# Output-projection weight sums: added in SBUF by accumulating DMAs, in place of DRAM

## The chip, the cores and the metric

One core of one Trainium2 chip. The metric is the device time of one launch in microseconds; the kernel before was run three times. All times in the trace are counted from the first instruction of one profiled execution.

## What is computed

A trunk of two layers on a residual stream h of 512 tokens by 2048 channels, all in float32:

```python
u = rms_norm(h, g_norm)
proj = u @ w_in                      # 2048 x 4096
...
y = jnp.concatenate([y_main, y_mem], axis=-1)     # 512 x 2048
h = h + y @ w_out                    # 2048 x 2048, in both layers
```

Layer A's main branch is a gated linear recurrence, layer B's is stick-breaking attention; both have a memory branch of four heads. Between them keys and values are projected from h. The change is in `y @ w_out` alone, with `w_out_a` in layer one (s = 0 in the code) and `w_out_b` in layer two (s = 1).

## The kernel before

Every float32 matmul is made of three passes over float32r operands: each operand is split in a high part (a rounding copy) and a low part (the rest), and TensorE adds high x high, high x low and low x high in PSUM (`three_passes`, L2126 to L2128).

The output projection uses products of sums instead of eight plain quadrant products. `w_out` is cut in two column pairs (n = 0, 1); each pair is a 2048 x 1024 matrix of quadrants b11, b12, b21, b22, each 1024 x 512. Beside the quadrants it needs four sums: t1 = b11 + b12, t2 = t1 + b22, t3 = b12 + b22, t4 = t2 + b21. Seven products per pair, each over two **slabs** of 512 x 512 weights (1 MB), make N_PROJ = 28 slabs per layer, 14 per pair, numbered u. The sums over the y tiles are made by VectorE in SBUF (`y_sum`, L1388).

Weight sums: in the GpSimd program, before its other work and again behind the V stores, `move` (L618) issues DRAM-to-DRAM DMAs, four of 512 KB for each 2 MB matrix, some plain and some accumulating, into `weight_sums`. For one pair they come in a fixed order: t1 and t3 get copies of b11 and b12, then b12 and b22 are added; t2 is copied from t1 and gets b22; t4 is copied from t2 and gets b21. GpSimd waits for `sums_made` between dependent steps. Two pairs, n = 0 and 1, are made in the first layer's time, n = 2 and 3 in the second's.

Slab loads: `load_proj` (L519) on SyncE's queue (SP) loads slab u, already a quadrant or a finished sum, in 2 KB rows (L533) to one of five raw slots of SBUF, by

```python
RAW = [(0, 1, 0, 1, 3, 4)[u] if u < 6 else (2, 3, 0, 1)[(u - 6) % 4] for u in range(N_PROJ)]
proj_raw = [w_raw[:, 0], w_raw[:, 1], four(5), four(6), four(1)]
```

Slots 0 and 1 are `w_raw`, the others parts of `work`. From slab 7 on a load waits until VectorE has finished (`lo_ready`) slab u - 4 (u - 3 for slab 7), the one that held its slot. `load_out` (L539) writes out the order of SP's queue: y tiles (`load_quad`, L537) stand between the slabs, slab 2 waits for the pair's sums, slab 14 for those of the second pair.

For each slab ScalarE (ACT) copies raw to `w_hi` in two halves (`proj_split`, L751; L755), once TensorE is done with slab u - 2, whose `w_hi` and `w_lo` it overwrites; VectorE (DVE) subtracts to `w_lo` (L1367, L1372); TensorE (PE) runs 24 matmuls. Both queues have other work between slabs, in a fixed order: splits of y tiles (L761, L1379), the residual's loads (issued by ACT, L1007 from in_x in layer one, L1246 from h_scratch in layer two), and the additions that drain PSUM. The h^T and V stores of the following stage are also on GpSimd's queue (`store_ht`, L625).

Of the kernel before, what the change touches and what calls it, by code (L numbers as in the profile page):

```python
# [51 lines left out]
RAW = [(0, 1, 0, 1, 3, 4)[u] if u < 6 else (2, 3, 0, 1)[(u - 6) % 4] for u in range(N_PROJ)]  # L52
# [25 lines left out]
def raw_loads(s, u):  # L78

    return s * RAW.count(RAW[u]) + RAW[:u + 1].count(RAW[u])  # L80

# [28 lines left out]
def trunk(nc, x, x_t, mem, mem_t, gain_cols, chan_cols, w_mem_kv, w_in_a, w_rec_gate, w_in_gate,  # L110
# [5 lines left out]
    wa, woa, wb, wob = w_in_a[0], w_out_a[0], w_in_b[0], w_out_b[0]  # L116
# [5 lines left out]
    sums_dram = nc.dram_tensor("weight_sums", [4, 4, KQ * P, C], F32, kind="Internal").ap()  # L122

    def weights(s, n):

        w = (woa, wob)[s]
        b11, b12, b21, b22 = (w[KQ * P * r:KQ * P * (r + 1), C * (2 * n + c):C * (2 * n + c + 1)]
                              for r in range(2) for c in range(2))
        return (b11, b12, b21, b22, *(sums_dram[2 * s + n, m] for m in range(4)))
# [15 lines left out]
    with ExitStack() as ctx:  # L145
# [3 lines left out]
        def sem(name):  # L149
            return ctx.enter_context(nc.semaphore(name))  # L150
# [37 lines left out]
        def four(n):  # L188
            return block(n).rearrange("p (b t) -> p b t", b=4)
# [37 lines left out]
        proj_raw = [w_raw[:, 0], w_raw[:, 1], four(5), four(6), four(1)]  # L227
# [199 lines left out]
        proj_loaded = [sem(f"proj_loaded{n}") for n in range(5)]  # L427
# [3 lines left out]
        sums_made = [sem(f"sums_made{n}") for n in range(4)]  # L431
# [16 lines left out]
        def _(sp):  # L448
# [70 lines left out]
            def load_proj(s, u):  # L519
                b11, _, b21, b22, t1, t2, t3, t4 = weights(s, u // 14)  # L520
                if u < 14:
                    w, c = ((b11, 0), (b11, 1), (t3, 0), (t3, 1), (b21, 0), (t4, 0), (b21, 1), (t4, 1),
                            (t1, 0), (t1, 1), (t2, 0), (t2, 1), (b22, 0), (b22, 1))[u]
                else:
                    order = ((t1, t3, b11, t2, b22, b21, t4), (t1, t2, b22, b11, b21, t3, t4))[s]
                    w, c = order[(u - 14) // 2], u % 2
# [6 lines left out]
                sp.dma_start(proj_raw[RAW[u]], w[C * c:C * (c + 1), :].rearrange("(k p) n -> p k n", p=P)  # L533
                             ).then_inc(proj_loaded[RAW[u]], 16)

# [3 lines left out]
            def load_out(s, y):  # L539
# [11 lines left out]
                sp.wait_ge(sums_made[2 * s], 16 * 32)  # L551
# [5 lines left out]
                load_proj(s, 5)  # L557
# [5 lines left out]
                sp.wait_ge(sums_made[2 * s + 1], 16 * 32)  # L563
# [39 lines left out]
        def _(pool):  # L603
# [48 lines left out]
            for n in range(4):  # L652
                b11, b12, b21, b22, t1, t2, t3, t4 = weights(n // 2, n % 2)
                if n == 2:
                    for c in range(2):
                        store_ht(c)
                    store_ht(3)
                    store_ht(2)
                    pool.wait_ge(h_squares, 12)
                    pool.wait_ge(h_stored, 48)  # L660
                    load_sums(0)
                    load_sums(1)
                    for step in range(KQ):
                        store_sums(step)
                    for m in range(4):
                        store_value(m)
                move(n, t1, b11, ALU.bypass)
                move(n, t3, b12, ALU.bypass)
                pool.wait_ge(sums_made[n], 16 * 8)
                move(n, t1, b12, ALU.add)  # L670
                move(n, t3, b22, ALU.add)
                pool.wait_ge(sums_made[n], 16 * 16)
                move(n, t2, t1, ALU.bypass)
                pool.wait_ge(sums_made[n], 16 * 20)
                move(n, t2, b22, ALU.add)
                pool.wait_ge(sums_made[n], 16 * 24)
                move(n, t4, t2, ALU.bypass)
                pool.wait_ge(sums_made[n], 16 * 28)
                move(n, t4, b21, ALU.add)
# [3 lines left out]
        def _(act):  # L683
# [67 lines left out]
            def proj_split(s, u):  # L751
                act.wait_ge(slab_done, U_PROJ[s] + u - 1)
                act.wait_ge(proj_loaded[RAW[u]], 16 * raw_loads(s, u))
                for k in (0, 2):
                    nc.scalar.activation(w_hi[:, u % 2, k:k + 2, :], proj_raw[RAW[u]][:, k:k + 2, :], ACT.Copy  # L755
                                         ).then_inc(hi_ready, 2)
# [555 lines left out]
        def _(dve):  # L1312
# [54 lines left out]
            def proj_split(s, u, hooks=()):  # L1367
                for k in (0, 2):
# [3 lines left out]
                    V.tensor_tensor(w_lo[:, u % 2, k:k + 2, :], proj_raw[RAW[u]][:, k:k + 2, :],  # L1372
# [1177 lines left out]
```

## Time and profile before

| | |
|---|---|
| median of three runs | 1468.76 us (1468.38 to 1469.23) |
| span of the profiled execution, first to last instruction | 1466.5 us |
| profiled execution's own time around the span | not given apart; the median stands 2.3 us above the span |
| busy: PE / DVE / ACT / POOL | 1458.0 / 997.5 / 716.3 / 122.8 us |
| share of 16 DMA engines: SP's queue, software (GpSimd), ACT's queue | 40.3% / 28.3% / 9.0% |
| moved by DMA | 357.97 MB, mean 244 GB/s |
| granted TensorE clock | 0.999 of full speed |
| output projection, layer one / layer two | about 461 to 632 us / 1292 to 1459 us |

A busy time is the union of an engine's instructions. A share of a queue is the time that its packets took, out of 16 engines' span. In a timeline "xN" is N instructions of one line that were merged, so that the us beside it are from the first one's start to the last one's end.

### The profile page before, as it was taken

The page shows a single profiled execution, that of the slowest core. Times are in us where ns is not written, and L with a number is a line of the kernel's source. Part 1 is how long each engine was busy: PE and PEld are TensorE (multiplying, and loading weights), DVE is VectorE, ACT ScalarE, POOL GpSimd, SP SyncE. Part 2 cuts the span into 40 slices and gives each one's busy share as a digit, 9 for nine tenths or more (in the row PEclk, how much of TensorE's full clock was granted, in tenths as well). Part 3 has the DMA queues.
Part 4 walks back from the last instruction along what each step waited for, and adds up shares of the span by engine and source line. Part 5 has one row for each costly group of instructions (what it writes and reads, how often), then busy time and mean ns, then how long its engine had stood idle before and what let it go on. Part 6 is the DMA issues. An engine that isn't in the chain of part 4 may idle for free.

```text
span 1466.5 us, 18207 instructions
## 1 busy us (share of the span) xinstructions
PE 1458.0 (99%) x6842; PEld 1221.7 (83%) x6842; DVE 997.5 (68%) x1317; ACT 716.3 (49%) x1066; POOL 122.8 (8%) x184
## 2 busy tenths in 40 slices
PE   9999999999999999999999999999999999999998
PEld 7888888888888888888888888888888888888886
DVE  6775568465576896856579676556566566578987
ACT  6764544444544645763325654433333433455465
POOL 0001111111110000000010001111111011000000
PEclk9999999999999999999999999999999999999999
DMA  9877788777886987477989876687888888858853
GB/s 344 290 287 225 159 215 228 174 235 158 212 251 165 323 323 260 155 262 282 358 326 372 291 224 219 244 218 196 230 241 244 202 239 208 226 188 329 315 200 144
DMA packets 154189, 357.97 MB, mean 244 GB/s; under 512 B 7824, under 2 KB 23440, under 8 KB 150032
## 3 DMA queue, kind: packets, MB, share of 16 engines
q1 hardware_dynamic: 103824, 205.98, 40.3%
q0 software_dynamic: 29376, 102.77, 28.3%
q10 hardware_dynamic: 20928, 48.41, 9.0%
q8 instruction: 38, 0.62, 0.2%
q14 instruction: 23, 0.19, 0.0%
HBM read 310.99 MB, written 113.25 MB: 289 GB/s over the span
## 4 chain that ended last, share of the span: by engine, by line
PE 99%; DMA 0%; SPq 0%; ACT 0%; issue 0%; DVE 0%; ACTq 0%
PE main L2128 25%; PE main L2127 25%; PE main L2126 25%; PE aux L2127 6%; PE aux L2126 6%; PE aux L2128 6%; PE aux L2484 2%; PE aux L2473 1%; DMA w_raw<-in_w_mem_kv 0%; PE aux L2270 0%; PE main L2178 0%; PE aux L2178 0%; PE main L2199 0%; PE main L2202 0%; PE main L2205 0%; PE aux L2220 0%
## 5 line engine op out<-in xcount | busy, mean ns | idle before, releaser
L2126 PE MATMUL main<-act_hi,w_hi 128*128 128x512 f32 x1216 | 475.3, 391 | 0.0
L2127 PE MATMUL main<-act_lo,w_hi 128*128 128x512 f32 x1216 | 473.6, 389 | 0.0
L2128 PE MATMUL main<-act_hi,w_lo 128*128 128x512 f32 x1216 | 473.6, 389 | 0.0
L2128 PEld LDWEIGHTS main<-act_hi,w_lo 128*128 128x128 f32 x1216 | 228.3, 188 | 47.4
L2127 PEld LDWEIGHTS main<-act_lo,w_hi 128*128 128x128 f32 x1216 | 228.4, 188 | 46.7
L2126 PEld LDWEIGHTS main<-act_hi,w_hi 128*128 128x128 f32 x1216 | 228.4, 188 | 46.4
L1334 DVE SCALAR_TENSOR_TENSOR w_lo<-w_raw,gains,w_hi 128x512 fp32r<-128x512 f32 x180 | 123.3, 746 | 120.5 <-ACT w_hi L704 120.5
L704 ACT ACTIVATE w_hi<-w_raw,gains 128x512 fp32r<-128x512 f32 x180 | 115.4, 712 | 140.6 <-PE main L2128 121.9
L1325 DVE TENSOR_TENSOR w_lo<-w_raw,w_hi 128x1024 fp32r<-128x1024 f32 x88 | 104.1, 1222 | 105.2 <-ACT w_hi L697 105.0
L697 ACT ACTIVATE w_hi<-w_raw 128x1024 fp32r<-128x1024 f32 x88 | 88.5, 1057 | 169.5 <-PE main L2128 132.7
L2126 PE MATMUL main<-w_hi,act_hi 128*128 128x512 f32 (+1 forms) x432 | 163.5, 378 | 0.0
L2127 PE MATMUL main<-w_lo,act_hi 128*128 128x512 f32 (+1 forms) x432 | 163.4, 378 | 0.0
L2128 PE MATMUL main<-w_hi,act_lo 128*128 128x512 f32 (+1 forms) x432 | 163.1, 377 | 0.0
L2126 PE MATMUL aux<-w_hi,act_hi 128*128 128x512 f32 (+1 forms) x348 | 129.4, 372 | 0.0
L2127 PE MATMUL aux<-w_lo,act_hi 128*128 128x512 f32 (+1 forms) x348 | 129.2, 371 | 0.0
L2128 PE MATMUL aux<-w_hi,act_lo 128*128 128x512 f32 (+1 forms) x348 | 128.9, 370 | 0.0
L2126 PEld LDWEIGHTS main<-w_hi,act_hi 128*128 128x128 f32 x432 | 81.3, 188 | 15.6
L2128 PEld LDWEIGHTS main<-w_hi,act_lo 128*128 128x128 f32 x432 | 81.2, 188 | 15.2
L2127 PEld LDWEIGHTS main<-w_lo,act_hi 128*128 128x128 f32 x432 | 81.3, 188 | 14.8
L755 ACT ACTIVATE w_hi<-work 128x1024 fp32r<-128x1024 f32 x56 | 56.3, 1053 | 64.2 <-issue 53.7
L755 ACT ACTIVATE w_hi<-w_raw 128x1024 fp32r<-128x1024 f32 x56 | 56.2, 1051 | 57.3 <-issue 57.3
L1372 DVE TENSOR_TENSOR w_lo<-w_raw,w_hi 128x1024 fp32r<-128x1024 f32 x56 | 66.2, 1220 | 25.7 <-ACT w_hi L755 25.6
(321 smaller groups left out, 1861.4 us busy)
## 6 DMA issues: line engine op xcount, KB each, us to landing
w_raw<-in_w_in_a SPq DMA_DIRECT2D x32, 1024.0 KB, 6.7
w_raw<-in_w_in_b SPq DMA_DIRECT2D x32, 1024.0 KB, 7.9
weight_sums<-in_w_out_a POOLq DMA_DIRECT2D x48, 512.0 KB, 7.0
weight_sums<-in_w_out_b POOLq DMA_DIRECT2D x48, 512.0 KB, 7.2
weight_sums<-weight_sums POOLq DMA_DIRECT2D x32, 512.0 KB, 6.4
w_raw<-weight_sums SPq DMA_DIRECT2D x16, 1024.0 KB, 6.6
work<-weight_sums SPq DMA_DIRECT2D x16, 1024.0 KB, 7.5
w_raw<-in_w_mem_kv SPq DMA_DIRECT2D x13, 1024.0 KB, 5.2
```

What stands on the lines that cost most here:

```text
L697: nc.scalar.activation(w_hi[:, j % 2, k:k + 2, :], raw[:, k:k + 2, :], ACT.Copy).then_inc(hi_ready, 2)
L704: nc.scalar.activation(w_hi[:, j % 2, k, :], raw[:, k, :], ACT.Copy, scale=s).then_inc(hi_ready, 1)
L755: nc.scalar.activation(w_hi[:, u % 2, k:k + 2, :], proj_raw[RAW[u]][:, k:k + 2, :], ACT.Copy).then_inc(hi_ready, 2)
L1325: V.tensor_tensor(w_lo[:, j % 2, k:k + 2, :], w_raw[:, j % 2, k:k + 2, :], w_hi[:, j % 2, k:k + 2, :].bitcast(F32), ALU.subtract).then_inc ...
L1334: V.scalar_tensor_tensor(lo, raw[:, k, :], gain[:, KS * j + k:KS * j + k + 1], hi, ALU.mult, ALU.subtract).then_inc(lo_ready, 1)
L1372: V.tensor_tensor(w_lo[:, u % 2, k:k + 2, :], proj_raw[RAW[u]][:, k:k + 2, :], w_hi[:, u % 2, k:k + 2, :].bitcast(F32), ALU.subtract).then ...
L2126: TE.matmul(o, a[0], b[0], start=first, stop=False)
L2127: TE.matmul(o, a[0], b[1], start=False, stop=False)
L2128: return TE.matmul(o, a[1], b[0], start=False, stop=final)
L2473: last = TE.transpose(o, beta[:, t, c:c + P], ident[:])
L2484: last = TE.matmul(aux[:, 0, P * k:T], v, w, start=(k, n) == order[0], stop=(k, n) == order[-1])
```

## The change

- The DRAM sums t1, t2 and t4 go. What stays in DRAM is t3 = b12 + b22 and a new w2 = b11 + b21, for the first pair of each layer, and t3 alone for the second pair of layer two, each made by two copies and two accumulating moves of 1 MB (`pair_sum`).
- The other sums are formed in the raw slots. A table SLABS gives for each slab (slot, what is loaded, what is added): "loaded" is a plain DMA on SP's queue, "added" an accumulating DMA on GpSimd's queue (`add_weights`), onto the load or, where nothing is loaded, onto what the slot still holds from the slab before in it. So t1 is b11 plus b12, t2 is the raw t1 plus b22, t4 is t3 plus w2 or t2 plus b21. GpSimd's queue holds the adds of a layer in the order of the slabs; those of layer one stand ahead of the h^T stores.
- There are four raw slots, not five. The order of the seven products is the same, and so is TensorE's work; the row halves of a matrix are taken in the order of HALVES.
- ACT waits for the load or for the add, whichever is a slab's last.
- The host lays out `w_out_a` and `w_out_b` so that each slab is one contiguous MB, 8 KB for each partition.

```diff
-RAW = [(0, 1, 0, 1, 3, 4)[u] if u < 6 else (2, 3, 0, 1)[(u - 6) % 4] for u in range(N_PROJ)]
+B11, B12, B21, B22, T3, W2 = range(6)
+HALVES = [(0, 1, 0, 1, 0, 0, 1, 1, 0, 1, 0, 1, 0, 1)[u] if u < 14 else u % 2 for u in range(N_PROJ)]
+
+FIRST_PAIR = ((0, B11, None), (1, B11, None), (0, T3, None), (1, T3, None), (3, B21, None), (0, None, W2),
+              (2, B21, None), (1, None, W2), (3, B11, B12), (0, B11, B12), (3, None, B22), (0, None, B22),
+              (2, B22, None), (1, B22, None))
+SLABS = (FIRST_PAIR + ((0, B11, B12), (3, B11, B12), (2, B12, B22), (1, B12, B22), (2, B11, None), (1, B11, None),
+                       (0, None, B22), (3, None, B22), (2, B22, None), (1, B22, None), (2, B21, None), (1, B21, None),
+                       (0, None, B21), (3, None, B21)),
+         FIRST_PAIR + ((3, B11, B12), (0, B11, B12), (3, None, B22), (0, None, B22), (2, B22, None), (1, B22, None),
+                       (2, B11, None), (1, B11, None), (2, B21, None), (1, B21, None), (2, T3, None), (1, T3, None),
+                       (3, None, B21), (0, None, B21)))
...
             def load_proj(s, u):
...
+                slot, base, _ = SLABS[s][u]
+                if base is None:
+                    return
                 if u == 4:
                     sp.wait_ge(ms_done, 4 * s + 4)
-                elif u < 4:
+                elif u < 2:
                     sp.wait_ge(lo_ready, 4 * (U_PROJ[s] + u - 1))
-                elif u >= 7:
-                    sp.wait_ge(lo_ready, 4 * (U_PROJ[s] + u - (2 if u == 7 else 3)))
...
+                elif u != 6:
+                    sp.wait_ge(lo_ready, 4 * (U_PROJ[s] + raw_before(s, u) + 1))
+                sp.dma_start(proj_raw[slot], weights(s, u // 14, base)[HALVES[u]].rearrange("p (k n) -> p k n", k=KS)
+                             ).then_inc(proj_loaded[slot], 16)
...
-            def move(n, dst, src, op):
-                for r in range(4):
-                    rows = slice(2 * P * r, 2 * P * r + 2 * P)
-                    pool.dma_start(dst[rows], src[rows], accum_op=op).then_inc(sums_made[n], 16)
+            def move(dst, src, op):
+                for c in range(2):
+                    pool.dma_start(dst[c], src[c], accum_op=op, max_dma_last_dim=8192).then_inc(sums_made, 16)
...
+            def add_weights(s, u):
+
+                slot, base, other = SLABS[s][u]
+                if base is None:
+                    pool.wait_ge(lo_ready, 4 * (U_PROJ[s] + raw_before(s, u) + 1))
+                else:
+                    pool.wait_ge(proj_loaded[slot], 16 * slab_moves(s, u, 1))
+                pool.dma_start(proj_raw[slot], weights(s, u // 14, other)[HALVES[u]].rearrange("p (k n) -> p k n", k=KS),
+                               accum_op=ALU.add).then_inc(proj_added[slot], 16)
...
             pool.wait_ge(sumsq_ready, NMB + NT)
...
+            pair_sum(0, 0, 0, T3, B12, B22)
+            pair_sum(4, 0, 0, W2, B11, B21)
+            add_all(0)
+            for c in range(2):
+                store_ht(c)
...
+            pair_sum(8, 1, 0, T3, B12, B22)
+            pair_sum(12, 1, 0, W2, B11, B21)
+            pair_sum(16, 1, 1, T3, B12, B22)
+            add_all(1)
...
             def proj_split(s, u):
                 act.wait_ge(slab_done, U_PROJ[s] + u - 1)
-                act.wait_ge(proj_loaded[RAW[u]], 16 * raw_loads(s, u))
+                slot, _, other = SLABS[s][u]
+                if other is None:
+                    act.wait_ge(proj_loaded[slot], 16 * slab_moves(s, u, 1))
+                else:
+                    act.wait_ge(proj_added[slot], 16 * slab_moves(s, u, 2))
```

`raw_before(s, u)` is the last slab before u in the same slot; `slab_moves` counts the loads or the adds of a slot so far.

## Rows read from the trace of the kernel before

**Rows 1.** The page: TensorE's busy time, and the DMA strip in 40 slices.
```profile
PE 1458.0 (99%) x6842; PEld 1221.7 (83%) x6842; DVE 997.5 (68%) x1317; ACT 716.3 (49%) x1066; POOL 122.8 (8%) x184
...
DMA  9877788777886987477989876687888888858853
```

**Rows 2.** The page: the chain that ended last.
```profile
PE 99%; DMA 0%; SPq 0%; ACT 0%; issue 0%; DVE 0%; ACTq 0%
```

**Rows 3.** Waits of TensorE: us in total, times, longest.
```profile
PE main L2188 <- POOL ones L604: 1.1, 1, 1.1
PE main L2199 <- ACT w_hi L800: 0.6, 1, 0.6
```

**Rows 4.** Timeline of ScalarE: start, us, line, out<-in, [idle before <-releaser].
```profile
497.90 2.01 ACT L755 ACTIVATE w_hi<-work 128x1024 fp32r<-128x1024 f32 x2 [3.43 <-issue]
...
525.10 1.06 ACT L755 ACTIVATE w_hi<-work 128x1024 fp32r<-128x1024 f32 x1 [1.53 <-issue]
525.15 0.38 ACTq L1007 DMA_DIRECT2D work<-in_x  x1
...
530.54 2.01 ACT L755 ACTIVATE w_hi<-work 128x1024 fp32r<-128x1024 f32 x2 [3.43 <-issue]
...
535.98 1.06 ACT L755 ACTIVATE w_hi<-w_raw 128x1024 fp32r<-128x1024 f32 x1 [1.53 <-issue]
...
563.18 1.06 ACT L755 ACTIVATE w_hi<-w_raw 128x1024 fp32r<-128x1024 f32 x1 [3.43 <-issue]
...
1361.34 2.02 ACT L755 ACTIVATE w_hi<-work 128x1024 fp32r<-128x1024 f32 x2 [3.42 <-issue]
...
1393.98 1.06 ACT L755 ACTIVATE w_hi<-w_raw 128x1024 fp32r<-128x1024 f32 x1 [2.21 <-issue]
```

**Rows 5.** Timeline of VectorE: slabs 2, 8, 9 and 11 of layer one.
```profile
485.29 2.35 DVE L1372 TENSOR_TENSOR w_lo<-w_raw,w_hi 128x1024 fp32r<-128x1024 f32 x2
...
515.38 2.36 DVE L1372 TENSOR_TENSOR w_lo<-w_raw,w_hi 128x1024 fp32r<-128x1024 f32 x2 [0.78 <-ACT w_hi L755]
...
522.38 2.35 DVE L1372 TENSOR_TENSOR w_lo<-w_raw,w_hi 128x1024 fp32r<-128x1024 f32 x2
...
532.84 2.35 DVE L1372 TENSOR_TENSOR w_lo<-work,w_hi 128x1024 fp32r<-128x1024 f32 x2
```

**Rows 6.** Timeline of SyncE's queue: start, us of issue, out<-in.
```profile
494.04 0.92 SPq L537 DMA_DIRECT2D work<-y_scratch  x2
...
529.34 6.24 SPq L533 DMA_DIRECT2D work<-weight_sums  x2
535.63 0.82 SPq L537 DMA_DIRECT2D f_raw<-y_scratch  x1
...
1360.15 0.37 SPq L533 DMA_DIRECT2D work<-weight_sums  x1
```

**Rows 7.** Windows: PE, PEld, DVE, ACT, POOL busy; granted clock, DMA share, GB/s.
```profile
494.00:533.60 39.60, 39.60 (x176) 32.80 (x175) 33.97 (x29) 21.28 (x23) 0.00 (x0) 1.00 0.92 336
1325.00:1364.40 39.40, 39.40 (x175) 32.63 (x175) 33.76 (x29) 21.09 (x23) 0.00 (x0) 1.00 0.91 333
509.00:520.00 11.00, 11.00 (x50) 9.13 (x49) 9.22 (x8) 6.04 (x7) 0.00 (x0) 1.00 1.04 391
```

**Rows 8.** Line L621: duration in ns, min/median/max; first and last start.
```profile
L621 POOL DMA_DIRECT2D weight_sums<-in_w_out_a x48: 557/888/1014, 116.8 to 455.1; - x48
```

**Rows 9.** Timeline of GpSimd: the first h store.
```profile
594.64 0.83 POOL L625 DMA_DIRECT2D ht_scratch<-f_raw  x1 [138.66 <-ACT f_raw L725]
```

**Rows 10.** DMA view, 142 to 200 us: queues; issues, us to landing.
```profile
q0 software_dynamic: 2137, 4.13, 47.3%
q1 hardware_dynamic: 2637, 5.24, 26.8%
...
weight_sums<-in_w_out_a POOLq DMA_DIRECT2D x8, 512.0 KB, 6.8
```

**Rows 11.** DMA view, 117.3 to 125.2 us: plain software moves.
```profile
q0 software_dynamic: 432, 1.57, 62.5%
```

More of the change, by code:

```diff
@@ L75, in in_column, with slab_moves, raw_before @@
     return (q // 2) * C + (q % 2) * DR if q < 2 * NPAIR else 2 * DR + (q - 2 * NPAIR) * C
-def raw_loads(s, u):
-    return s * RAW.count(RAW[u]) + RAW[:u + 1].count(RAW[u])
+def slab_moves(s, u, part):
+    slot = SLABS[s][u][0]
+    return sum(SLABS[q][v][part] is not None for q in range(2) for v in range(N_PROJ)
+               if SLABS[q][v][0] == slot and (q, v) <= (s, u))
+def raw_before(s, u):
+    return max((v for v in range(u) if SLABS[s][v][0] == SLABS[s][u][0]), default=None)
 class Chain:
@@ L120, in trunk, with weights @@
     h_v = h_dram.rearrange("(t p) n -> p t n", p=P)
[L122 to L129, printed above, removed]
+    sums_dram = nc.dram_tensor("weight_sums", [2, 2, 2, 2, P, KS * C], F32, kind="Internal").ap()
+    def weights(s, n, q):
+        return (w_out_a, w_out_b)[s][n, q] if q < 4 else sums_dram[s, n, q - 4]
     ht_dram = nc.dram_tensor("ht_scratch", [NK, P, T], F32, kind="Internal").ap()
@@ L426, in trunk @@
         scale_ready = sem("scale_ready")
[L427 removed]
+        proj_loaded = [sem(f"proj_loaded{n}") for n in range(4)]
+        proj_added = [sem(f"proj_added{n}") for n in range(4)]
         k1_loaded = [sem(f"k1_loaded{n}") for n in range(2)]
@@ L430, in trunk @@
         q22_loaded = [sem(f"q22_loaded{n}") for n in range(2)]
-        sums_made = [sem(f"sums_made{n}") for n in range(4)]
+        sums_made = sem("sums_made")
         sum_ready = sem("sum_ready")
@@ L616, in _, with pair_sum, add_all @@
                                     pattern=[[-1, P]], channel_multiplier=1).then_inc(const_ready, 1)
-            def move(n, dst, src, op):
-                for r in range(4):
-                    rows = slice(2 * P * r, 2 * P * r + 2 * P)
-                    pool.dma_start(dst[rows], src[rows], accum_op=op).then_inc(sums_made[n], 16)
+            def move(dst, src, op):
+                for c in range(2):
+                    pool.dma_start(dst[c], src[c], accum_op=op, max_dma_last_dim=8192).then_inc(sums_made, 16)
+            def pair_sum(before, s, pair, total, first, second):
+                a, b, t = (weights(s, pair, q) for q in (first, second, total))
+                if before:
+                    pool.wait_ge(sums_made, 16 * before)
+                move(t, a, ALU.bypass)
+                pool.wait_ge(sums_made, 16 * (before + 2))
+                move(t, b, ALU.add)
+            def add_weights(s, u):
[6 more added lines that the diff above has]
+                               accum_op=ALU.add).then_inc(proj_added[slot], 16)
+            def add_all(s):
+                for u in range(N_PROJ):
+                    if SLABS[s][u][2] is not None:
+                        add_weights(s, u)
             def store_ht(c):
@@ L651, in _ @@
             pool.wait_ge(sumsq_ready, NMB + NT)
[L652 to L679, printed above, removed]
+            pair_sum(0, 0, 0, T3, B12, B22)
[3 more added lines that the diff above has]
+                store_ht(c)
+            store_ht(3)
+            store_ht(2)
+            pool.wait_ge(h_squares, 12)
+            pool.wait_ge(h_stored, 48)
+            load_sums(0)
+            load_sums(1)
+            for step in range(KQ):
+                store_sums(step)
+            for m in range(4):
+                store_value(m)
+            pair_sum(8, 1, 0, T3, B12, B22)
+            pair_sum(12, 1, 0, W2, B11, B21)
+            pair_sum(16, 1, 1, T3, B12, B22)
+            add_all(1)
         @blk.scalar
```

28 lines of the change are left out of this document (11 added, 17 removed).

## The prediction

> **What bounds the kernel now.** I read the page's shares first: TensorE (PE) is busy in 99% of the span and the strip of the DMA engines stands at 7 to 9 tenths for most of it [rows 1]. The chain that ended last is TensorE at 99% [rows 2], and its table of waits has two entries, 1.1 and 0.6 us, both in the first 12 us [rows 3]. So TensorE never waits after its start. Nothing that only makes a DMA or GpSimd (POOL) idle can win time; the change can only keep the time or make weights late. The question is whether the 28 slabs of each output projection still come in time.
>
> A slab is split by ScalarE (ACT, L755) when the slab two before it is done. Splits start 5.44 us apart (530.54, 535.98) and take 2.01 us for both halves [rows 4]; VectorE (DVE, L1372) follows with 2.35 us [rows 5]. The first half of slab u must be through both, 1.06 + 1.2 us, when TensorE ends slab u-1, 5.44 us after the split could start. So a split may be 3.1 us late before TensorE stands. That slack is real: ACT stands idle for 1.5 to 3.4 us before these splits.
>
> Now the DMA engines in this stage. From 494.0, when the last y tiles of the first layer are fetched [rows 6], to 533.6 (slab 11's latest split, 530.54 + 3.1) they are already busy for 0.92 of the time with 336 GB/s; the same stretch of layer two, 1325.0 to 1364.4, shows 0.91 and 333. Inside it 509 to 520 is full: 391 GB/s at a share of 1.04 [rows 7]. That is the price of a plain MB slab (1.049 MB / 391 GB/s): **2.7 us of all 16 engines**.
>
> **The change, part by part.** (1) Removed: 128 half-MB DRAM-to-DRAM moves on GpSimd's queue: those that read in_w_out_a are issued from 116.8 to 455.1 us [rows 8], as many again for layer two. TensorE covers them entirely, so their removal is worth nothing; likewise the 8 and 12 moves of 1 MB that stay in the same stages. The h and V stores that share this queue lose nothing: the last add of layer one waits for VectorE's read of slab 21, whose split comes four slabs after the one at 563.18, at 584.9, plus 3.5 us for the read [rows 4], and the first h store was issued at 594.64 [rows 9]. If adds run late, that store is late with TensorE and still far ahead of its readers in the V stage.
>
> (2) Loads: by the table SLABS, of 28 MB slabs per layer only 20 are plain loads now. At 8 KB pieces instead of 2 KB I expect no faster rate than 391 GB/s: between nothing and a tenth, covered by the range.
>
> (3) Added: 14 accumulating DMAs of 1 MB into SBUF in layer one (6 in the first pair of quadrant columns, 8 in the second), 12 in layer two (6, 6). **What is one worth?** No row shows an accumulate into SBUF. The nearest is the add DRAM-to-DRAM in 2 KB pieces: in 142 to 200 the software queue moved 4.13 MB (eight adds of 512 KB) in 47.3% of 58 us, so 7.0 us of all engines per MB slab, while plain loads beside them took 3.1 (26.8% for 5.24 MB) [rows 10]. Plain software moves in 117.3 to 125.2 cost 3.3 (62.5% of 7.9 us for 1.57 MB) [rows 11]. An add thus costs about two copies (7.0 / 3.3 = 2.1), as if both inputs passed the same engine. Bounds: 2.7 us (the read of SBUF is free) and 7.0 us (as in DRAM, no gain from long pieces). I take twice a plain slab into SBUF, **5.4 us**, nearest to the ratio of the rows. In latency, a 512 KB add landed in a median of 6.8 us, 3.5 of it engine time, so 3.3 fixed: an undisturbed 1 MB add lands in 5.4 + 3.3 = 8.7 us.
>
> (4) New waits. GpSimd adds in order of slabs; each add of a loaded slab waits for that load, each add onto an old slab for VectorE's last read. Behind a late add stand all later adds, and for it waits ACT, which has y splits and the drains of PSUM queued behind; SP's later loads wait for VectorE in turn. The shortest turn is slabs 10 and 11, which add onto 8 and 9: VectorE is through with 8 at 517.74 and with 9 at 524.73 [rows 5]; latest splits are 525.10 + 3.1 = 528.2 and 533.6 [rows 4]. That leaves 10.5 and 8.9 us for 8.7 us, so almost nothing for traffic beside it. Raw slot 4 goes: slab 5 now adds into slot 0 once VectorE is through with slab 2, 485.29 + 2.35 = 487.6 [rows 5], and lands about 496.4, before its split at 497.90 [rows 4]: no cost. SP's waits move only with the slots.
>
> **The sum**, as a balance of DMA time. First pair, layer one, from 494.0: the add of slab 7 (queued behind 5's) and those of 8, 9, 10, 11 make 5 x 5.4 = 27.0. Plain: y tiles 1 MB (two halves), slabs 6, 8, 9, 12, 13, the residual's first two in_x loads, issued in slabs 7 and 8, and half of the third, at 525.15 [rows 4, 6]: 8.5 x 2.7 = 23.0. Together 50.0, so slab 11 is ready at 544.0, against 533.6: **+10.4**. Layer two has the same schedule and in place of in_x the h_scratch loads: 1325.0 + 50.0 against 1364.4: **+10.6**.
> Second pair, layer one, all times 10.4 later: slab 14's load starts when VectorE is through with 11, 532.84 + 2.35 + 10.4 = 545.6 [rows 5]. Due by slab 17's latest split, 563.18 + 3.1 + 10.4 = 576.7: four adds 21.6, plain slabs 14 to 17, the 1 MB y tile of 535.63 and one in_x, 6 x 2.7 = 16.2, together 37.8, so 583.4: **+6.7**. The rest (adds 20, 21, 26, 27 into slots that were read six slabs before, plain loads) has room, ten slabs of 5.44 us. Layer two may start this pair when slab 10 is read, 1360.15 + 10.6 [rows 6], and has 36.9 us for the same 37.8 (split 17 at 1393.98 [rows 4]): +0.9, which I count as 0.
> Sum 10.4 + 10.6 + 6.7 = 27.7 us on the span of 1466.5. The median of the runs, 1468.76, stands 2.3 us above that span, so 1496. I round down by 2 for the pieces of 8 KB (plain slabs 0.1 us cheaper each, some 20 of them in the balances): **1494 us**.
>
> **The rivals.**
> *A. In time after all: 1469 (1468.4 to 1469.5).* The second read is hidden and an add costs 2.7: first balance 13.5 + 23.0 = 36.5 us against 39.6, second 27.0 against 31.1; adds land in 6 us, under 8.9. For it: no row of an SBUF target. Against: the factor 2.1 between add and copy. This ends on the other side, not slower; it decides below 3.3 us per add ((39.6 - 23.0) / 5).
> The Trainium skill's page "DMA: Bandwidth & Descriptors" (section "Anatomy of one DMA — SWDGE (gpsimd) path") fits any software DMA as 2.0 us plus bytes / 436e3, without a word on accumulating; 1 MB would then be 4.4 us, and the time as in A, estimated by that page. The rows speak against it: 512 KB would land in 3.2, and they show 6.8.
> *B. Latency only: 1474.* The engines overlap adds and loads better than my sum has it (full stretches show a share over 1), but four adds onto slabs two back (10 and 11 of both layers) come 1 to 2 us late: +5.
> *C. Full price of DRAM adds, 7.0: 1526.* First balances 58.0, so +18.4 and +18.6; second 44.2, so +13.1 (31.1 us there) and +7.3 (36.9): +57.4 on the span. For it: it is the only add that the rows show. Against: part of its time may be DRAM's, and the 2 KB pieces'.
> *D. Faster, under 1466.* TensorE's idle time after 12 us is nil and its pace is set by the matmuls; only noise gives this.
>
> **How the numbers follow.** Forecast 0.48 (alone 1480 to 1510), C 0.14, B 0.14, A 0.21, D 0.03. About 0.2% (3 us) is what a measurement of this kernel can tell from no change. Slower by more: 0.48 + 0.14 + 0.14 = 0.76; within: 0.21; faster: 0.03. A's low end and C's sum with some room give 1468 to 1527.
>
> **What would show it.** TensorE waiting at L2126 for w_lo, first at slabs 8 to 11 of both layers, ACT's splits waiting for DMAs from in_w_out_a or in_w_out_b, adds with 9 us and more from issue to landing, a DMA share of 1.0 from about 496 to 545, and a software queue with 5 to 6 us of 16 engines per add. The granted clock stays at 1.00 [rows 7]. An add near 3 us, or a table of TensorE's waits as short as now, would make the forecast wrong; so would TensorE's lost time lying outside the projections.

## The result and the profile after

The changed kernel takes **1520.72 us** (median of four runs, 1519.62 to 1524.8) where the kernel before, beside it on the same chip, takes 1468.99 (1468.38 to 1470.22): a ratio of 1.0357, 95% interval 1.0345 to 1.037. It is 52 us slower; 25 had been forecast. The profiled execution has a span of 1518.4 us, 51.9 more than before. One execution of the last variant below, 2094.44 us at a granted clock of 0.654, was in a slow state and does not count in that variant's ratio.

The page of the kernel after: busy times, the DMA strip, the chain that ended last.

```profile
PE 1473.5 (97%) x6842; PEld 1228.5 (81%) x6842; DVE 998.1 (66%) x1317; ACT 716.6 (47%) x1066; POOL 67.6 (4%) x102
...
DMA  9878524242345999667999875888423334479973
...
PE 86%; DMA 10%; DVE 3%; ACT 1%; issue 1%; SPq 0%; DVEq 0%; ACTq 0%
```

The matmuls are the same 6842, yet the chain is no longer TensorE alone [rows 1, 2]: a tenth of it is DMA. The waits of TensorE in the kernel after (us in total, times, longest):

```profile
PE main L2156 <- DVE w_lo L1402: 26.1, 6, 7.6
PE aux L2156 <- DVE w_lo L1402: 9.7, 5, 6.3
```

Eleven waits, 35.8 us, stand where before there was none after 12 us [rows 3]. Another 15.5 of the 51.9 us are in TensorE's busy time, of which more below, and 0.6 in gaps too short for the table. Where the loss builds up is read from ScalarE's splits of the slabs. Timeline of ScalarE after, slabs 8, 11, 13, 17, 18, 19, 20 of layer one, then 14, 15, 16 and 17 of layer two (start, us, line, [idle before <- releaser]):

```profile
522.98 1.06 ACT L785 ACTIVATE w_hi<-work 128x1024 fp32r<-128x1024 f32 x1 [9.60 <-DMA work<-in_w_out_a]
...
543.10 2.01 ACT L785 ACTIVATE w_hi<-w_raw 128x1024 fp32r<-128x1024 f32 x2 [3.80 <-DMA w_raw<-in_w_out_a]
...
551.47 1.06 ACT L785 ACTIVATE w_hi<-w_raw 128x1024 fp32r<-128x1024 f32 x1 [2.57 <-issue]
...
586.63 2.01 ACT L785 ACTIVATE w_hi<-w_raw 128x1024 fp32r<-128x1024 f32 x2 [3.26 <-DMA w_raw<-in_w_out_a]
...
598.78 2.00 ACT L785 ACTIVATE w_hi<-work 128x1024 fp32r<-128x1024 f32 x2 [8.24 <-DMA work<-in_w_out_a]
...
605.16 2.01 ACT L785 ACTIVATE w_hi<-w_raw 128x1024 fp32r<-128x1024 f32 x2 [2.15 <-DMA w_raw<-in_w_out_a]
...
609.39 1.06 ACT L785 ACTIVATE w_hi<-w_raw 128x1024 fp32r<-128x1024 f32 x1 [2.23 <-issue]
...
1421.76 1.06 ACT L785 ACTIVATE w_hi<-work 128x1024 fp32r<-128x1024 f32 x1 [6.69 <-DMA work<-in_w_out_b]
...
1435.09 2.00 ACT L785 ACTIVATE w_hi<-w_raw 128x1024 fp32r<-128x1024 f32 x2 [11.32 <-DMA w_raw<-in_w_out_b]
...
1443.02 2.01 ACT L785 ACTIVATE w_hi<-work 128x1024 fp32r<-128x1024 f32 x2 [5.93 <-DMA work<-in_w_out_b]
...
1447.72 2.01 ACT L785 ACTIVATE w_hi<-w_raw 128x1024 fp32r<-128x1024 f32 x2 [1.47 <-DMA w_raw<-in_w_out_b]
```

Set against the same splits of the kernel before ([rows 4] and their neighbours), these lines date the loss. A split may be 3.1 us late without harm, so what is lost for good is read where a split again starts on time for its own TensorE (releaser "issue"):

| us later than before | layer one | layer two |
|---|---|---|
| at the start of the projection | 0.0 | 29.9 |
| at slab 11 | 12.6 | 43.5 |
| at slab 13 (first pair done) | 10.1 | 40.8 |
| at slab 17 | 23.5 | 53.7 |
| at slab 19 | 31.1 | 51.9 |
| from slab 21 on | 29.9 | 51.9 |

So four stretches carry all of it: **first pairs +10.1 and +10.9, second pairs +19.8 and +11.1**. Between the projections nothing is won or lost. These are the shares of this one execution; how far they hold in others is taken up with the adds in the first pairs only.

What an add costs: the DMA view of the kernel after, 494 to 544 us (queue: packets, MB, share of 16 engines).

```profile
q0 software_dynamic: 766, 5.49, 53.9%
q1 hardware_dynamic: 1771, 6.29, 31.9%
q10 hardware_dynamic: 1424, 2.85, 15.9%
```

The shares sum to 1.02: the engines are full. GpSimd's queue used 53.9% of 50 us for 5.49 MB, which is **5.15 us of 16 engines for an add of 1 MB** (1.049 million bytes); plain loads beside it used 31.9% for 6.29 MB, 2.66 us each.

The windows of the kernel after (PE, PEld, DVE, ACT, POOL busy; granted clock, DMA share, GB/s), and two matmuls in the last of them:

```profile
520.00:530.00 10.00, 4.86 (x13) 3.55 (x12) 5.79 (x5) 2.00 (x2) 0.86 (x1) 0.71 1.01 288
...
1430.00:1440.00 10.00, 2.44 (x6) 1.96 (x7) 3.69 (x4) 2.00 (x2) 0.86 (x1) 0.61 1.02 294
```

```profile
1437.56 0.79 PE L2156 MATMUL main<-w_hi,act_hi 128*128 128x512 f32 x1 [7.57 <-DVE w_lo L1402]
1438.15 0.63 PE L2157 MATMUL main<-w_lo,act_hi 128*128 128x512 f32 x1
```

The granted clock falls below 1.00 in these windows. Where it does, as here behind 7.6 us of standing, matmuls take 0.63 us against 0.39 elsewhere: the lower level, 1.2 GHz, for 7 to 10 us at a time. This happens at five places in the projections, each time behind a wait of 4.9 to 7.6 us, and this is where TensorE's busy time grows from 1458.0 [rows 1] to 1473.5 us.

### The profile page after: what moved, and what is told of

Read it like the earlier page. It is cut to its first block, busy times and chain, and to the rows that moved or that the text cites. A ratio compares the mean times of both kernels' runs of the same rounds, so it can differ in the third digit from the quotient of the medians.

```text
span 1518.4 us, 18108 instructions
## 1 busy us (share of the span) xinstructions
PE 1473.5 (97%) x6842; PEld 1228.5 (81%) x6842; DVE 998.1 (66%) x1317; ACT 716.6 (47%) x1066; POOL 67.6 (4%) x102
## 4 chain that ended last, share of the span: by engine, by line
PE 86%; DMA 10%; DVE 3%; ACT 1%; issue 1%; SPq 0%; DVEq 0%; ACTq 0%
PE main L2156 23%; PE main L2157 23%; PE main L2158 23%; DMA work<-in_w_out_a 5%; PE aux L2156 4%; PE aux L2157 4%; PE aux L2158 4%; DMA work<-in_w_out_b 2%; DVE w_lo L1402 2%; DMA w_raw<-in_w_out_b 2%; PE aux L2514 1%; PE aux L2503 1%; ACT w_hi L785 1%; PE aux L2300 0%; DMA f_raw<-in_mem_t 0%
## 5 line engine op out<-in xcount | busy, mean ns | idle before, releaser
L2156 PE MATMUL main<-w_hi,act_hi 128*128 128x512 f32 (+1 forms) x432 | 168.3, 390 | 26.2 <-DVE w_lo L1402 26.1
L1355 DVE TENSOR_TENSOR w_lo<-w_raw,w_hi 128x1024 fp32r<-128x1024 f32 x88 | 104.1, 1222 | 105.3 <-ACT w_hi L723 105.2
L723 ACT ACTIVATE w_hi<-w_raw 128x1024 fp32r<-128x1024 f32 x88 | 88.5, 1057 | 170.3 <-PE main L2158 132.7
L2157 PE MATMUL main<-w_lo,act_hi 128*128 128x512 f32 (+1 forms) x432 | 166.9, 386 | 0.0
L2158 PE MATMUL main<-w_hi,act_lo 128*128 128x512 f32 (+1 forms) x432 | 166.2, 385 | 0.0
L785 ACT ACTIVATE w_hi<-w_raw 128x1024 fp32r<-128x1024 f32 x64 | 64.2, 1051 | 86.6 <-issue 29.0
L1402 DVE TENSOR_TENSOR w_lo<-w_raw,w_hi 128x1024 fp32r<-128x1024 f32 x64 | 75.6, 1220 | 42.3 <-ACT w_hi L785 42.0
L1402 DVE TENSOR_TENSOR w_lo<-work,w_hi 128x1024 fp32r<-128x1024 f32 x48 | 56.6, 1220 | 48.0 <-ACT w_hi L785 47.7
```

The source lines that it names most:

```text
L723: nc.scalar.activation(w_hi[:, j % 2, k:k + 2, :], raw[:, k:k + 2, :], ACT.Copy).then_inc(hi_ready, 2)
L785: nc.scalar.activation(w_hi[:, u % 2, k:k + 2, :], proj_raw[slot][:, k:k + 2, :], ACT.Copy).then_inc(hi_ready, 2)
L1355: V.tensor_tensor(w_lo[:, j % 2, k:k + 2, :], w_raw[:, j % 2, k:k + 2, :], w_hi[:, j % 2, k:k + 2, :].bitcast(F32), ALU.subtract).then_inc ...
L1402: V.tensor_tensor(w_lo[:, u % 2, k:k + 2, :], proj_raw[SLABS[s][u][0]][:, k:k + 2, :], w_hi[:, u % 2, k:k + 2, :].bitcast(F32), ALU.subtra ...
L2156: TE.matmul(o, a[0], b[0], start=first, stop=False)
L2157: TE.matmul(o, a[0], b[1], start=False, stop=False)
```

## The experiments

The kernel before was run beside each; its medians lay between 1468.57 and 1468.81 us. Line numbers differ by a few between the kernels.

**Copies in place of adds.** One argument of the DMA is changed; the software DMAs and all their waits stay. This kernel leaves the sums out: a slab holds its second matrix alone.

```diff
-                               accum_op=ALU.add).then_inc(proj_added[slot], 16)
+                               accum_op=ALU.bypass).then_inc(proj_added[slot], 16)
```

> The 26 adds become plain software copies of the same bytes, in the same places and behind the same waits; the sums of the weights are left out, so the output is another. Theory 1 (an add costs the 16 engines about 5.1 us per MB slab, twice a copy, and this is what fills the DMA time): a copy costs 2.7, both projections fit again, 1469 to 1474 us. Theory 2 (GpSimd's queue is the cost: adds in order, each behind a load or a read, slow software issue): the waits stay, 1500 us or more.

Measured: 1476.78 us, ratio 1.0072 (1.0049 to 1.0096). Its waits of TensorE, then its DMA view, 494 to 544 us:

```profile
PE main L2156 <- DVE w_lo L1402: 2.2, 1, 2.2
PE aux L2156 <- DVE w_lo L1402: 2.0, 1, 2.0
```

```profile
q1 hardware_dynamic: 2154, 8.48, 43.7%
q0 software_dynamic: 720, 5.24, 25.8%
```

A copy on the same queue costs 2.58 us per MB (25.8% of 50 us, 5.24 MB), half an add. With copies 44 of the 52 us are gone; queue, waits, issue and the number of slots together make 8 at most. The time is 3 us above the range of Theory 1 and far below that of Theory 2. It is also 8 us above the 1469 us of rival A, who had reckoned with adds at the price of a copy: in the profiled execution 4.7 us are lost at slabs 14 to 19 of layer one, where that balance saw room.

**The layout alone.** The kernel before, with the slabs laid out in stretches of 8 KB and its DRAM moves in 1 MB with 8 KB pieces:

```diff
-                for r in range(4):
-                    rows = slice(2 * P * r, 2 * P * r + 2 * P)
-                    pool.dma_start(dst[rows], src[rows], accum_op=op).then_inc(sums_made[n], 16)
+                for r in range(2):
+                    pool.dma_start(dst[r], src[r], accum_op=op, max_dma_last_dim=8192).then_inc(sums_made[n], 16)
```

> The kernel before with one part of the change alone: w_out in 8 KB stretches and the DRAM sums made by moves of 1 MB in pieces of 8 KB; no add into SBUF. Theory 1: TensorE never waited for these loads, so 1469 us as before; a DRAM add should cost about 5.1 us of 16 engines per MB and not 7.0. Theory 2 (long pieces themselves crowd out the other queues): some slabs late, over 1472.

Measured: 1469.36 us, ratio 1.0018 (0.9999 to 1.0036). Long stretches win nothing here, where TensorE had no load to wait for; three of the ten executions took 1473 to 1479 us. The DRAM adds did get cheaper, as expected: from 132.7 to 168.5 us the software queue took 57.0% for 4.19 MB, 5.1 us per MB where it had been 7.0 [rows 10]. The profiled execution had one new wait of TensorE, far from the projections, at 249 us:

```profile
PE aux L2123 <- DVE xc_lo L1721: 3.9, 1, 3.9
```

Here all later splits are 5.2 us late, more than the wait, and the matmuls behind it take 0.62 us. It is taken up again with the last two variants below.

**The urgent loads first.** In the kernel after GpSimd issues the adds of slabs 20 and 21 (and 17 before them) before SyncE issues the loads of 18 and 19, which are needed sooner. Timeline of GpSimd after, then of SyncE's queue after:

```profile
575.68 1.75 POOL L650 DMA_DIRECT2D w_raw<-in_w_out_a  x2 [1.89 <-DMA w_raw<-in_w_out_a]
581.52 0.86 POOL L650 DMA_DIRECT2D work<-in_w_out_a  x1 [4.09 <-issue]
```

```profile
584.91 0.33 SPq L545 DMA_DIRECT2D work<-in_w_out_a  x1
590.18 0.33 SPq L545 DMA_DIRECT2D w_raw<-in_w_out_a  x1
```

The experiment holds the two adds back until both loads have landed:

```diff
+                    if s == 0 and u in (20, 21):
+                        for v in (18, 19):
+                            pool.wait_ge(proj_loaded[SLABS[s][v][0]], 16 * slab_moves(s, v, 1))
```

> The changed kernel, but layer one's adds of slabs 20 and 21 wait until the loads of slabs 18 and 19 have landed. Theory 1a (adds that run ahead take the engines from the urgent plain loads, which then land in 14 instead of 6 us): slab 18's split comes about 6 us earlier, 1512 to 1516 in all. Theory 1b (only the total of DMA work counts): the lost time moves to slab 20, within 2 us of 1521.

Measured: 1521.58 us, ratio 1.0363 (1.0346 to 1.0381), as the kernel after. Its ScalarE timeline, slabs 18, 19 and 20:

```profile
595.15 2.01 ACT L788 ACTIVATE w_hi<-work 128x1024 fp32r<-128x1024 f32 x2 [2.13 <-DMA work<-in_w_out_a]
...
599.81 2.01 ACT L788 ACTIVATE w_hi<-w_raw 128x1024 fp32r<-128x1024 f32 x2 [0.42 <-DMA w_raw<-in_w_out_a]
...
610.50 2.00 ACT L788 ACTIVATE w_hi<-w_raw 128x1024 fp32r<-128x1024 f32 x2 [8.68 <-DMA w_raw<-in_w_out_a]
```

Slabs 18 and 19 come 3.6 and 5.4 us earlier than in the kernel after (598.78, 605.16), slab 20 waits for its add in their place (8.68 us idle at ScalarE), and the end is as late. Order within the queues is not the cause; there is too much work for the DMA engines up to that point.

**Does the lower clock cost?** 40 matmuls on old data, into a bank that is overwritten, are put in ahead of the waits at slabs 8, 14 and 18 of layer one and 8 of layer two:

```diff
+                    if (s, u) in ((0, 8), (0, 14), (0, 18), (1, 8)):
+                        k_all, tok = place(slot)
+                        for n in range(40):
...
+                            TE.matmul(banks[:, 0, 0:HALF], act_hi[:, k, tok.start:tok.start + P], act_hi[:, k, tok],
+                                      start=True, stop=True)
```

> The changed kernel with 40 matmuls of 256 columns (about 4.8 us, their sums are overwritten by the next product) on TensorE ahead of its longest waits: slabs 8, 14 and 18 of layer one and slab 8 of layer two. Theory K (TensorE's clock is halved for 6.8 us because it stood idle for over 5 us, and each time costs about 3 us): no half clock at these four, about 12 us less, 1506 to 1511. Theory L (the half clock has another reason or costs nothing because the weights are the limit there): 1519 to 1524.

Measured: 1520.85 us, ratio 1.0361 (1.0343 to 1.0378). The same two windows in this kernel:

```profile
520.00:530.00 10.00, 9.37 (x61) 8.40 (x60) 4.56 (x3) 2.01 (x2) 0.86 (x1) 1.00 1.02 288
...
1430.00:1440.00 10.00, 7.43 (x32) 5.51 (x30) 4.72 (x4) 1.92 (x3) 0.87 (x1) 1.00 1.04 296
```

The clock is back at 1.00 in both, the mean over the span 0.996 against 0.986, and the time is unchanged. The lower clock costs nothing here that four runs can tell (the interval is 2.5 us to either side): the weights come when the DMA engines have them, and a slower matmul only fills time that TensorE would stand. So the split of the 51.9 us in 35.8 of waits and 15.5 of longer matmuls is one of appearance; it is late weights that cost.

**Adds in the first pairs only, adds in the second pairs only.** The sums of the other pairs are made in DRAM as before, so that their slabs are plain loads. The tables of layer one:

```diff
# first pairs only
+SECOND = ((T1, T3, B11, T2, B22, B21, T4), (T1, T2, B22, B11, B21, T3, T4))
+SLABS = tuple(FIRST_PAIR + tuple(((0, 3, 2, 1)[u % 4], order[u // 2], None) for u in range(14)) for order in SECOND)
# second pairs only
+FIRST_PAIR = tuple(zip((0, 1, 0, 1, 3, 0, 2, 1, 3, 0, 2, 1, 3, 0),
+                       (B11, B11, T3, T3, B21, T4, B21, T4, T1, T1, T2, T2, B22, B22), (None,) * 14))
+SLABS = (FIRST_PAIR + ((1, B11, B12), (2, B11, B12), (3, B12, B22), (0, B12, B22), (3, B11, None), (0, B11, None),
+                       (1, None, B22), (2, None, B22), (3, B22, None), (0, B22, None), (3, B21, None), (0, B21, None),
+                       (1, None, B21), (2, None, B21)),
```

> Adds into SBUF for the first pair of quadrant columns of each layer alone (6 and 6 adds); the second pair's four sums are made in DRAM again, in 8 KB pieces, and loaded plainly. Theory W: only the first balances stay, +10 in each layer (that is what the changed kernel shows until slab 13), 1488 to 1492. Theory S (a start of delay is what makes the second pairs late, and plain loads suffer too): 1500 or more.

> Adds into SBUF only for the second pair of slabs of each layer (the first pair's sums are made in DRAM by short pieces, as before). Theory W2, each pair has its own balance: in layer one the DMA engines have, from 535.2 us, six adds of 5.15 us (30.9) and ten plain MB of 2.7 us (27.0), 57.9 us in all, so slab 19 would be split at about 593.1 where the kernel before splits it at 577.2, 16 us late; in layer two slab 15's own add costs between nothing and 11 us. So 1485 to 1496 us, with PE waits on the splits of 16 to 27 us. Rival, backlog: the second pairs are late only because the first pair left its transfers behind; without adds in the first pair they have room, the splits end at most 5 us late in either layer, and the time is under 1478 us.

First pairs only: 1500.66 us, ratio 1.0205 (1.0181 to 1.023). Its waits of TensorE:

```profile
PE main L2161 <- DVE w_lo L1407: 18.3, 3, 6.7
PE aux L2161 <- DVE xc_lo L1759: 7.3, 1, 7.3
PE aux L2161 <- DVE w_lo L1407: 2.6, 3, 1.1
```

In the profiled execution, 38.5 us longer than before, the second pairs lose nothing in either layer; layer two's first pair costs 11.5 (10.9 in the kernel after), layer one's 17.9 (10.1), and 9.0 are lost ahead of the projections, 7.3 of it the wait for xc_lo. The time lies in Theory S's range, but what S says isn't seen, as no second pair loses anything; what W had at nothing is the 9.0 us and a first pair that costs 17.9 in place of 10. That surplus can be followed. VectorE's timeline of this kernel:

```profile
546.30 1.23 DVE L1661 TENSOR_TENSOR work<-work 128x1024 f32<-128x1024 f32 x1 [7.72 <-DMA work<-in_x]
```

VectorE's additions for the residual stand in its queue ahead of slab 9's subtraction, and they wait for the first in_x load. That load took 28.3 us here against 11.1 in the kernel after, so slab 9 is read late and the add of slab 11 onto it starts late. It isn't a matter of this variant: the run below that holds back loads 18 and 19 of layer two has layer one's code unchanged, and in its profiled execution the load took 29.9 us, VectorE waited 8.4 us for it, the add of slab 11 was issued at 543.98 in place of 534.61, and the first pair cost **19.8 us where the kernel after lost 10.1**. Why this load takes 11 us in one execution and 30 in another stays open.

Second pairs only: 1491.62 us, ratio 1.0162 (1.0144 to 1.0181). Its waits of TensorE, its DMA view, 535 to 592 us, and ScalarE's split of slab 19:

```profile
PE main L2164 <- DVE w_lo L1410: 9.7, 3, 4.8
PE aux L2164 <- DVE w_lo L1410: 6.0, 2, 5.6
```

```profile
q0 software_dynamic: 864, 6.29, 53.0%
q1 hardware_dynamic: 1937, 7.61, 35.2%
q10 hardware_dynamic: 1007, 3.00, 13.5%
```

```profile
591.84 4.11 ACT L793 ACTIVATE w_hi<-w_raw 128x1024 fp32r<-128x1024 f32 x4 [3.42 <-DMA w_raw<-in_w_out_a]
```

Here the first pair is on time to the end (0.9 us early throughout), and still the second pair of layer one costs 16.0 us and that of layer two 7.3. Its expectation had slab 19 at 593.1 and 16 us late: the split starts at 591.84, and the shares sum to 1.02 over 57 us. So the second pairs are late **by their own load**. The rest, 3.8 us in each layer (19.8 - 16.0, 11.1 - 7.3), goes with the adds of the first pair, but in layer one it is not a fixed amount: with the same code the profiled execution of the next run lost 16.4 there. That it is a backlog is argued, not shown.

In layer two these adds are late one by one. GpSimd's timeline of this kernel, the add of slab 16 of layer two, and ScalarE's, its split:

```profile
1398.85 0.86 POOL L660 DMA_DIRECT2D work<-in_w_out_b  x1 [11.40 <-DVE w_lo L1410]
```

```profile
1410.87 2.00 ACT L793 ACTIVATE w_hi<-work 128x1024 fp32r<-128x1024 f32 x2 [7.74 <-DMA work<-in_w_out_b]
```

Slab 16 adds onto slab 14: issued at 1398.85 when VectorE had read 14, ready 12.0 us later, on full engines. Undisturbed adds land in 8.1 to 8.9 us (slabs 26 and 27).

**Layer two's loads 18 and 19 held back.** In the kernel after slab 15's add takes from 1419.43 to its split at 1435.09, 15.7 us, beside two loads that are not urgent. They are held until it has landed:

```diff
+                if s == 1 and u == 18:
+                    sp.wait_ge(proj_added[SLABS[s][15][0]], 16 * slab_moves(s, 15, 2))
```

> The changed kernel, but in layer two the loads of slabs 18 and 19 are held until slab 15's add has landed. Theory P (slab 15 is late by 8 us because loads that are not due yet, 18, 19 and final_norm, share the engines with its add, which took 15.6 us to land in place of 8.7): slab 15 comes about 4 to 5 us earlier and some of it stays, 1516 to 1519. Theory W (the sum of DMA work of the layer decides, order does not): the loss moves to slabs 18 and 19, 1520 to 1523.

Measured: 1525.14 us, ratio 1.037 (1.0348 to 1.0393). That is 2 us above the range of W and 6 above P's. The profiled execution loses 23.1 us in layer two, the kernel after 22.0: slab 15 comes 1.4 us earlier, where P had 4 to 5, and slab 17 comes 1.9 us later. As in layer one, reordering only moves the wait. This execution's longer time is in layer one, whose code is unchanged: 36.2 us lost there against 29.9.

**Half of each add.** The adds take only the first two of a slab's four parts, so that the sums of the other two are left out; this makes their pieces 4 KB.

```diff
-                pool.dma_start(proj_raw[slot], weights(s, u // 14, other)[HALVES[u]].rearrange("p (k n) -> p k n", k=KS),
+                pool.dma_start(proj_raw[slot][:, 0:2, :],
+                               weights(s, u // 14, other)[HALVES[u]].rearrange("p (k n) -> p k n", k=KS)[:, 0:2, :],
```

> The changed kernel with each of the 26 adds over half of its slab (512 KB; the other half of the sums is left out). Theory W: an add then takes about 2.6 us of 16 engines, what a full copy took, and the projections nearly fit, 1469 to 1478. Rival (what costs is that there is an accumulate at all, with its waits, order and its hold on the engines): 1490 or more.

Measured: 1484.19 us, ratio 1.0102 (1.0085 to 1.0119). DMA view, 494 to 544 us:

```profile
q0 software_dynamic: 720, 2.62, 27.9%
```

Half the bytes cost 2.8 us of 16 engines per slab (27.9% of 50 us for five), about the 2.58 of a copy, and 36.5 of the 52 us are gone: the loss goes with the bytes added. But it is 7.4 us slower than the copies, which use the engines nearly as long, and that fits neither expectation. (The runs tell little more than that it is slower: the copies took 1473.87 to 1484.38, the half adds 1482.78 to 1487.01.) It isn't the latency on quiet engines, where the half adds of slabs 26 and 27 landed in 5.5 and 6.5 us and the copies in 6.7 and 5.9; the cause stays open.

**The adds in pieces of 4 KB.** The same adds in full, with pieces of 4 KB in place of 8 KB:

```diff
-                               accum_op=ALU.add).then_inc(proj_added[slot], 16)
+                               accum_op=ALU.add, max_dma_last_dim=4096).then_inc(proj_added[slot], 16)
```

> The changed kernel with the adds into SBUF in pieces of 4 KB, not 8 KB. Theory W (two passes through the engines whatever the piece): about 5.3 us of 16 engines per MB, 1517 to 1526; the other queues get a larger share beside an add, so in_x and slabs land earlier and adds later, without a gain in all. Rival (an add costs per piece, as much as in the DRAM moves of before, 7.0 us at 2 KB, so 6 at 4 KB): 1535 or more.

Measured: 1568.45 us, ratio 1.0681 (1.0663 to 1.0698), 48 us more again. DMA view, 494 to 544 us, and GpSimd's timeline, the adds of slabs 8, 9 and 10:

```profile
q0 software_dynamic: 1099, 4.24, 43.9%
```

```profile
513.29 1.21 POOL L650 DMA_DIRECT2D work<-in_w_out_a  x1 [14.78 <-issue]
527.01 1.21 POOL L650 DMA_DIRECT2D w_raw<-in_w_out_a  x1 [12.51 <-issue]
538.25 1.21 POOL L650 DMA_DIRECT2D work<-in_w_out_a  x1 [10.03 <-issue]
```

The time lies in the rival's range, but not for its reason: the price is 5.43 us per MB, hardly above 5.15, as Theory W had it. What is new is the releaser "issue" after 10 to 15 us of idle time: GpSimd waits for no semaphore, and each of these adds is issued 0.3 us after the one before it has landed, so that one is in flight at a time. No theory had that. Yet the kernel before shows it too, at its DRAM adds of half a MB in 2 KB pieces, here one of 142 to 200 us:

```profile
149.89 0.92 POOL L621 DMA_DIRECT2D weight_sums<-in_w_out_a  x1 [6.82 <-issue]
```

Common to both is not the size of a piece but, by these counts, the number of pieces in one add, 256. Adds of 128 pieces go three at a time: in the kernel after those of slabs 16, 17 and 20 are in flight together, and the fourth is issued at 581.52, 0.3 us after the first of them has landed; the half adds, also in 4 KB pieces, do the same (issued at 560.08, 562.81 and 563.34, the next at 566.35).

**Adds where there is room.** All sums in DRAM but those of the last two slabs of each layer, 26 and 27, with four raw slots; first with the DRAM moves in 8 KB pieces, then in half MB and 2 KB pieces:

```diff
+                                 (T1, T1, T3, T3, B11, B11, T2, T2, B22, B22, B21, B21, None, None),
+                                 (None,) * 12 + (B21, B21))),
```

```diff
-                    pool.dma_start(dst[c], src[c], accum_op=op, max_dma_last_dim=8192).then_inc(sums_made, 16)
+                    for h in (slice(0, 64), slice(64, 128)):
+                        pool.dma_start(dst[c][h], src[c][h], accum_op=op, max_dma_last_dim=2048).then_inc(sums_made, 16)
```

> Four raw slots and 8 KB stretches, but only t4 of the second pair is formed in SBUF (slabs 26 and 27 of each layer, onto t2); all other sums in DRAM. Theory W: the DMA engines are a third to a half idle from slab 20 on, 4 adds x 5.1 us fit, 1468 to 1471. Rival (any add beside the loads makes some slab late): 1474 or more.

> The kernel with t4 of the second pairs alone formed in SBUF, as in the run before, but the DRAM moves in pieces of 2 KB and half an MB each. Theory G (the 3 to 5 us above the kernel before come from the gate weights of the second recurrence group, whose short packets land in 19 us beside long DRAM adds, 12.5 beside short ones): no wait of TensorE there, 1468 to 1470. Rival (the four slab adds or the four slots cost it): 1472 or more.

The first: 1472.78 us, ratio 1.0025 (1.0013 to 1.0038), between its two expectations; the second **1468.22**, ratio 0.9997 (0.9987 to 1.0007), which is the time of the kernel before. In both the projections lose nothing: late adds on quiet engines are free. An add of the first kernel there, in its DMA view of 592 to 632 us:

```profile
work<-in_w_out_a POOLq DMA_DIRECT2D x1, 1024.0 KB, 8.9
```

What remained in the first was one wait at 250 us. The cause is in the DMA view of 215 to 262 us, the load of the gate weights (KB, us to landing), in the kernel before, then in the first, then in the second:

```profile
work<-in_w_in_gate ACTq DMA_DIRECT2D x1, 256.0 KB, 12.5
```

```profile
work<-in_w_in_gate ACTq DMA_DIRECT2D x1, 256.0 KB, 19.3
```

```profile
work<-in_w_in_gate ACTq DMA_DIRECT2D x1, 256.0 KB, 10.8
```

Beside DRAM adds of 8 KB pieces this small load takes 7 us longer and TensorE stands for it (3.4 us here, 3.9 in the layout experiment, 7.3 with first pairs only); with 2 KB pieces the wait is gone. The Trainium skill's page "DMA: Bandwidth & Descriptors" (section "Queues, rings and completion order") has each DMA engine take turns between its queues packet by packet; by that rule a queue of long packets gets more of the engine against one of short packets, and these three rows agree. They do not prove it: the 8 KB moves are also 1 MB each, of which three were in flight when this load was issued, against one at a time of the adds in 2 KB pieces, and no run separates the two.

No variant beats the kernel before.

## Why the prediction was right in kind and wrong in size

**What bounds the kernel, removals, other work:** right. The moves that went were covered; the stretches between the projections take as long as before. The h store left later with its slab, to no harm.

**The price of an add:** right, 5.4 forecast, 5.15 measured. The ratio of add to copy in DRAM [rows 10, 11] carries over to SBUF: 5.15 / 2.58 = 2.0. The latency of 8.7 is right too (8.9 above). By the fit of the Trainium skill's page "DMA: Bandwidth & Descriptors" (section "Anatomy of one DMA — SWDGE (gpsimd) path"), an estimate of 4.4 us for any software DMA of 1 MB, it would be half of that; the measurement decides. Rival A falls with the price. Rival B falls: the loss is bandwidth, since halving the bytes of the adds takes 36.5 us away. Rival C's total of 1526 is closer than the forecast, but for a wrong reason: its 7.0 us did not occur, and in DRAM too the price goes to 5.1 with 8 KB pieces.

**First pairs:** the balance was right, +10.4 and +10.6 forecast, +10.1 and +10.9 measured. That layer one comes within 0.3 us is luck all the same: another execution of the same code lost 19.8 there. The check of turns at slabs 10 and 11 left out that VectorE waits for the residual's in_x load before it reads slab 9.

**Second pair of layer one, the step that failed first.** +6.7 was forecast by a balance up to slab 17, and "the rest (adds 20, 21, 26, 27 ..., plain loads) has room". The term was mis-sized, +19.8 measured, and two errors are in it. At slab 17 the split came at 586.63, not at 583.4: 3.2 us more. And the balance was ended too early: behind slab 17 the engines stay full, with the adds of 20 and 21, the loads of 18 and 19, and a 2 MB store of h_scratch. Taken on to slab 19 by the prediction's own method, from 545.6: adds 14 to 17, 20 and 21, 6 x 5.15 = 30.9; plain, slabs 14 to 19, the y tile, one in_x and the store of 2 MB, 10 x 2.7 = 27.0; ready at 603.5, against a latest split of 574.06 + 3.1 + 10.4 = 587.6, so +16. Measured: 605.16. Only adds 26 and 27 have room, as the last variants show. Second pairs alone give the same 16.0, so most of it is this load and not what the first pair left. The copies show the same step: at half the price they still lose 4.7 us at these slabs. (That store, 2 MB in 9.4 us before, took 25.9 us: the prediction did not name it at all.)

**Second pair of layer two, the other failed step.** The balance left +0.9, "which I count as 0", and looked at slab 17 alone. Its "same 37.8" holds only because the loads of 18 and 19, which run early, stand in for those of 16 and 17, which layer two does not have; the 1 MB of final_norm is not in it. What decides, as far as the timelines show, is a path: slab 15's load cannot start before VectorE has read slab 11; then its add; 16 adds onto 14 and 17 onto 15 when those have been read. The adds of 14, 15 and 16 took 12.0, 15.6 and 17.3 us on full engines, not 8.7. The prediction had made that check, turn by turn, for slabs 10 and 11, and not here. Measured: +11.1, of which 7.3 remain without the first pair's adds.

Together the two are worth 19.8 + 11.1 - 6.7 - 0 = 24.2 us. With the 2 us taken off for 8 KB pieces, which did not show (a plain MB took 2.66 us beside the adds and 2.70 beside the copies, where 2.6 had been reckoned), this is the difference of 26.7 between forecast and result, but for 0.5.

**What would show it:** the waits at TensorE, ScalarE's splits behind DMAs, adds above 9 us and the share of 1.0 all came as said (the first wait, of 0.6 us, is already at slab 6, whose plain load is 3.3 us late; the first long one is at slab 8). "The granted clock stays at 1.00" was wrong: 0.61 to 0.76 in five windows; it cost nothing that can be told from the noise, as the filler matmuls show.

## What to carry to other kernels

An accumulating DMA into SBUF costs the DMA engines twice a copy, so it saves nothing against a plain load of a sum that was made earlier in quiet time; put it where the DMA strip has room, as at slabs 26 and 27. When two stretches that overload one resource follow each other, carry the balance on until the resource is idle, counting stores and work that isn't yet urgent, and do not stop at the last slab that looks tight. Holding back transfers on full engines, tried twice here, moved the wait from one slab to the next and left the end where it was. And before one execution's timeline is taken as the size of a loss, look at a second one of the same code: the first pair of layer one cost 10.1 us in one and 19.8 in another.

## What the runs showed of the hardware

- Adds of 256 pieces go one at a time: of 1 MB in 4 KB pieces into SBUF, GpSimd standing 10 to 15 us before issuing each of those shown, in a kernel that is 48 us slower at nearly the same engine time per MB, and of half a MB in 2 KB pieces in DRAM. Of adds of 128 pieces three were in flight (1 MB in 8 KB pieces, half a MB in 4 KB pieces), and the fourth was issued 0.3 us after the first had landed.
- An add costs 5.15 us of 16 engines per MB into SBUF in 8 KB pieces and 5.43 in 4 KB pieces; in DRAM 5.1 in 8 KB pieces and 7.0 in 2 KB pieces. A software copy into SBUF costs 2.58.
- Beside DRAM adds of 1 MB in 8 KB pieces a short load of 256 KB took 19.3 us, not 12.5; with half a MB and 2 KB pieces it took 10.8.
- In the kernel after, TensorE's granted clock is at half for 7 to 10 us behind each of five waits of 4.9 to 7.6 us, here without a cost that shows, since it waits for weights anyway.
